# A two-block transformer on one core: the sparse attention's key split on other engines, smaller inverses, and its mask inside another product

## The chip, the cores and the metric

The kernel runs on one core of a Trainium2 chip. The metric is the device time of one execution in microseconds (us). Five engines work at the same time, each through its own list of instructions in order: TensorE (PE; its weight loads are shown as PEld), VectorE (DVE), ScalarE (ACT), GpSimd (POOL) and SyncE (SP), which here only issues DMAs. They wait for one another through semaphores.

## What is computed

Two transformer blocks on 1024 tokens of width 1024 in float32. The first has a short convolution, a retention layer and an MLP. The second has two attentions side by side, whose outputs are gated, merged and followed by another MLP. The change lies wholly in the first of the two, the sparse one; the dense one (`mla_attention`) shares its loop.

```python
def one_block(bi):                      # 128 queries, 8 heads of 64; keys and values shared by the heads
    dots = einsum('bqhd,bsd->bqhs', iqb, ikf) * IDX_DIM ** -0.5
    score = where(causal, einsum('bqh,bqhs->bqs', iwb, relu(dots)), -inf)
    _, sel = top_k(score, 256)
    k_sel, v_sel = take_rows(k, sel), take_rows(v, sel)
    bias = rel_table[rel_bucket(posq[:, :, None] - take_rows(positions, sel))]
    logits = einsum('bqhd,bqkd->bqhk', qb, k_sel) * A_HEAD_DIM ** -0.5 + swapaxes(bias, 2, 3)
    logits = where(valid[:, :, None, :], logits, NEG_INF)
    p = softmax(logits, axis=-1)
    return einsum('bqhk,bqkd->bqhd', p, v_sel)
```

The kernel does not gather: it takes the product of the queries with all keys, adds -1e30 where a key was not selected, and goes on as in a dense attention.

## The kernel before

**The loop.** Both attentions run as one loop over 128 tiles, n = 0 to 127 (`ATT`). Tiles 0 to 63 are the dense attention: for each of four pairs of heads (a round of 16 tiles), the eight query blocks b of 128 queries, two heads each. Tiles 64 to 127 are the sparse one: for each query block b, eight tiles of 16 queries by 8 heads (128 rows); a tile is 128b + 16(r + 1) keys wide, r = 0 to 7. Tile n = 64 + 8b is the first of block b.

**One tile**, by engine, each engine in its own order:
- TensorE at step n: `logits(n + 1)` into two PSUM banks (after exp n - 1 has freed them and, for the sparse ones, after the comparisons of n + 1 are there), at odd n `attend_pair((n - 3) // 2)`, then `probs_t(n)`, the transposition of the probabilities (after exp n).
- VectorE: at n >= 64 `steps_of(n + 1)`, four comparisons of the positions (`STEP`, line 2425) from which TensorE makes the relative bias; at odd n `sums_inverted` (line 2397), the inverses of two tiles' row sums; the row maximum of tile n (`NMX`, line 2464); every fourth n `attended_scaled`, which scales the finished outputs (`YB` line 2406, `YA` line 2416).
- ScalarE: exp of tile n with its row sums (line 1765), the copy of the transposed probabilities of n - 1 (line 1746), every fourth n the copy `RBS` of the spread inverses (line 1753).

**Sparse logits** (lines 1297 to 1305). The float32 product is made of float32r parts. `QS` holds for each of 64 query tiles the high parts in rows 0 to 63 and the low parts in rows 64 to 127. `KHH` holds the high parts of the keys twice, `KLO` the low parts twice. Each chunk of up to 512 keys takes three products: QS with KHH, QS with KLO, and the selection `SELB` with the mask `MB` (both bfloat16), which brings the -1e30 of a query to its 8 heads. Then follow 12 products for the bias, of 32 columns of weights each.

**Setting up the sparse part.** At its step n = 52 (`KEYS_AT`) VectorE waits until 48 tiles have logits (the keys' tiles lie where heads 0 to 5 were), copies `AKB` into both halves of KHH (lines 2450, 2451), subtracts for both halves of KLO (line 2454), and makes the comparisons of tile 64. GpSimd moves the queries into QS: after the logits of tile 47 three quarters of them (`s_aq`; two subtractions, line 849, and two copies, line 853), after those of tile 63 the rest (`s_aq2`). TensorE's `logits(64)` waits for the keys (`s_kparts`) and for `s_aq`. GpSimd has nothing else to do in the loop.

**Inverses.** `sums_inverted` writes each of two row-sum columns 64 times side by side, a 128x128 tile `RINV`, and TensorE transposes that (line 862, `RINV`) at the end of `attend_pair`, so that the inverses stand along the columns, those of the first tile in PSUM rows 0 to 63, those of the second in 64 to 127.

## Time and profile before

| | |
|---|---|
| three runs | 2951.71, 2955.83, 2956.42 us (median 2955.83) |
| the profiled execution | 2956.02 us, of which span of the trace 2954.2 us |
| PE busy | 2833.2 us, 96% of the span |
| DVE busy | 1550.5 us, 52% |
| POOL busy | 1011.7 us, 34% |
| ACT busy | 721.1 us, 24% |
| dense attention, tiles 0 to 63 | 1648 to about 1821 us |
| sparse attention, tiles 64 to 127 | about 1821 to 2030 us |

The span in 40 slices of 73.9 us; each digit is the busy share of a slice in tenths, PEclk the granted TensorE clock in tenths:

```profile
PE   7999999999999999999999996999899999999997
DVE  4853234643333324657999457996454333333337
ACT  5001124432011113453211663443111100011101
PEclk9999999999999999999999997999999999999998
```

How to read it: the attention loop lies in slices 23 to 28 (counted from 1). Elsewhere VectorE is idle for more than half of the time; here it is as busy as TensorE, and the one slice with a lower clock and a less busy TensorE in the middle of the program (the 25th, 1773 to 1846 us) belongs to it.

### The profile page before, as it was taken

Reading aid. Unit: us, or ns where it says so; the run is one execution under the profiler, and the core shown is the slowest. Engines: PE = TensorE matmul, PEld = TensorE weight load, DVE = VectorE, ACT = ScalarE, POOL = GpSimd, SP = SyncE. Lnnn points to the kernel's source line nnn. Section 1 sums busy time; section 2 is a strip of 40 time slices with the busy share of each in tenths; the row PEclk is TensorE's granted clock in tenths of the full one; section 3 lists DMA queues with packets and bytes.
Section 4 is the critical chain, followed back from the end, with each engine's and each line's share of the span. In section 5 each row is a group of like instructions: output and inputs, shape, how many; then the busy total and the mean of one; then the engine's idle time right before and its main releaser. Section 6 shows DMA issues by size and latency. Waiting matters only on the chain.

```text
span 2954.2 us, 35848 instructions
## 1 busy us (share of the span) xinstructions
PE 2833.2 (96%) x14659; PEld 2262.4 (77%) x14676; DVE 1550.5 (52%) x1841; ACT 721.1 (24%) x1055; POOL 1011.7 (34%) x441
## 2 busy tenths in 40 slices
PE   7999999999999999999999996999899999999997
PEld 4888888778888887776886564566787888888886
DVE  4853234643333324657999457996454333333337
ACT  5001124432011113453211663443111100011101
POOL 1533224454444444441222113001344444444441
PEclk9999999999999999999999997999999999999998
DMA  8531113322111122352232000003311111111111
GB/s 302 190 103 38 41 43 130 91 87 85 50 50 43 49 77 87 93 161 57 61 100 79 15 1 1 2 2 108 135 43 50 43 50 50 50 48 44 50 50 64
DMA packets 253975, 208.64 MB, mean 71 GB/s; under 512 B 23051, under 2 KB 238618, under 8 KB 253466
## 3 DMA queue, kind: packets, MB, share of 16 engines
q1 hardware_dynamic: 250826, 198.50, 21.8%
q10 hardware_dynamic: 3024, 8.39, 0.7%
q8 instruction: 89, 1.46, 0.2%
q14 instruction: 36, 0.29, 0.0%
HBM read 184.84 MB, written 20.97 MB: 70 GB/s over the span
## 4 chain that ended last, share of the span: by engine, by line
PE 78%; DVE 16%; ACT 2%; issue 2%; DMA 0%; POOL 0%; SPq 0%; ACTq 0%; DVEq 0%; POOLq 0%
PE PS L1128 18%; PE PS L1138 17%; PE PS L878 13%; PE PS L1074 10%; DVE MB L2320 6%; PE PS L1090 5%; PE PS L1363 3%; PE PS L862 3%; PE PS L1281 2%; PE PS L1332 2%; DVE STEP L2425 1%; PE PS L1305 1%; PE PS L1192 1%; DVE NMX L2464 1%; PE PS L1297 0%
## 5 line engine op out<-in xcount | busy, mean ns | idle before, releaser
L754 POOL TENSOR_TENSOR WHI<-RAW,ZERO 128x1024 fp32r<-128x1024 f32 x144 | 277.1, 1924 | 1189.0 <-PE PS L1138 292.2
L767 POOL TENSOR_TENSOR WLO<-RAW,WHI 128x1024 fp32r<-128x1024 f32 x112 | 269.8, 2409 | 478.6 <-ACT WHI L1486 478.6
L756 POOL TENSOR_TENSOR WLO<-RAW,WHI 128x1024 fp32r<-128x1024 f32 x144 | 397.0, 2757 | 11.3
L878 PE MATMUL PS<-H,WHI 128*128 128x512 f32 x864 | 271.4, 395 | 10.0 <-DVE L L1820 7.9
L878 PE MATMUL PS<-L,WHI 128*128 128x512 f32 x864 | 268.3, 392 | 0.0
L878 PE MATMUL PS<-H,WLO 128*128 128x512 f32 x864 | 267.8, 391 | 0.0
L1600 ACT ACTIVATE RL<-PS 128x1024 f32<-128x1024 f32 x48 | 49.3, 1027 | 870.9 <-PE PS L1128 870.9
L2231 DVE TENSOR_TENSOR FT<-RL 128x1024 f32<-128x1024 f32 x48 | 92.8, 1934 | 316.3 <-ACT RL L1600 316.3
L1486 ACT ACTIVATE WHI<-RAW 128x1024 fp32r<-128x1024 f32 x112 | 118.7, 1060 | 468.3 <-PE PS L1074 198.2
L1074 PE MATMUL PS<-H,WHI 128*128 128x512 f32 x512 | 202.8, 396 | 2.5 <-POOL WLO L767 1.9
L1074 PE MATMUL PS<-H,WLO 128*128 128x512 f32 x512 | 200.3, 391 | 0.0
L1074 PE MATMUL PS<-L,WHI 128*128 128x512 f32 x512 | 200.1, 391 | 0.0
L878 PEld LDWEIGHTS PS<-H,WHI 128*128 128x128 f32 x864 | 161.7, 190 | 46.1 <-issue 10.7
L878 PEld LDWEIGHTS PS<-L,WHI 128*128 128x128 f32 x864 | 163.3, 189 | 34.9
L878 PEld LDWEIGHTS PS<-H,WLO 128*128 128x128 f32 x864 | 163.3, 189 | 34.6
L2320 DVE TENSOR_SCALAR_CACHE_REDUCE MB<-SCO,CAND 128x384 bf16<-128x384 f32 (+2 forms) x198 | 174.3, 943 | 1.2
L2244 DVE TENSOR_TENSOR F2SUM<-F2SUM,PS 128x2048 f32<-128x2048 f32 x28 | 64.1, 2288 | 186.4 <-PE PS L1138 186.4
L1128 PE MATMUL PS<-A2H,WHI 128*128 128x512 f32 x512 | 157.8, 389 | 1.4 <-issue 1.4
L1138 PE MATMUL PS<-F2H,WHI 128*128 128x512 f32 x512 | 157.7, 389 | 1.3 <-ACT RS L1786 1.3
L1128 PE MATMUL PS<-A2L,WHI 128*128 128x512 f32 x512 | 157.7, 389 | 0.0
L1138 PE MATMUL PS<-F2H,WLO 128*128 128x512 f32 x512 | 157.6, 389 | 0.0
L1138 PE MATMUL PS<-F2L,WHI 128*128 128x512 f32 x512 | 157.6, 389 | 0.0
(352 smaller groups left out, 5488.6 us busy)
## 6 DMA issues: line engine op xcount, KB each, us to landing
RAW<-w_fc SPq DMA_DIRECT2D x96, 512.0 KB, 3.9
RAW<-w_ff SPq DMA_DIRECT2D x64, 512.0 KB, 3.8
RAW<-w_in SPq DMA_DIRECT2D x62, 512.0 KB, 4.2
ADA<-w_ada SPq DMA_DIRECT2D x32, 512.0 KB, 5.4
RAW<-w_out SPq DMA_DIRECT2D x24, 512.0 KB, 4.0
ADA_FIRST<-w_ada SPq DMA_DIRECT2D x16, 512.0 KB, 9.4
X<-x_scratch SPq DMA_DIRECT2D x2, 4096.0 KB, 12.7
GB<-gate_scratch SPq DMA_DIRECT2D x8, 1024.0 KB, 5.3
```

The costliest lines, as they stand in the source:

```text
L754: nc.gpsimd.tensor_add(WHI[j][:, 0:n], RAW[j][:, 0:n], ZERO[:, 0:1].to_broadcast([P, n])).then_inc(s_whi, 1)
L756: nc.gpsimd.tensor_sub(WLO[j][:, 0:n], RAW[j][:, 0:n], WHI[j][:, 0:n].bitcast(F32)).then_inc(s_w, 1)
L767: nc.gpsimd.tensor_sub(WLO[w % 2][:, :], RAW[w % 2][:, :], WHI[w % 2][:, :].bitcast(F32)).then_inc(s_w, 1)
L862: return nc.tensor.transpose(dst, src, ident[0:n, 0:n])
L878: last = mm(bank(b + t), wt[:, k, :], a[:, k * S + t * HALF:k * S + (t + 1) * HALF], start=(k == 0 and n == 0), stop=(k == KC - 1 and n == 2))
L1074: last = mm(bank(w_bank(w)), wt[:, k, :], half(a, k, e), start=(k == 0 and n == 0), stop=(k == KC - 1 and n == 2))
L1090: last = mm(bank(w_bank(w) + c), wt[:, k, c * P:(c + 1) * P], half(a, k, e), start=(k == 0 and n == 0), stop=(k == 3 and n == 2))
L1128: last = mm(bank(b + t), wt[:, k, :], a[:, k * S + t * HALF:k * S + (t + 1) * HALF], start=(k == 0 and n == 0), stop=(k == KC - 1 and n == 2))
L1138: last = mm(bank(b + 2 * c + t), wt[:, k, c * P:(c + 1) * P], a[:, k * S + t * HALF:k * S + (t + 1) * HALF], start=(k == 0 and n == 0), st ...
L1486: A(WHI[w % 2][:, :], RAW[w % 2][:, :], ACT.Copy).then_inc(s_whi, 1)
L2231: V.tensor_tensor(FT[:, :], RL[i % 2][:, :], RL[i % 2][:, :], ALU.mult).then_inc(s_h32, 1)
L2320: V.tensor_scalar(mask(b), scores(b), CAND[:, b - 2:b - 1].bitcast(F32), 0.0, op, ALU.add, accum_out=REACH[:, b - 2:b - 1]).then_inc(s_dve, 1)
```

## The change

It has three parts, all in the attention loop.
1. The split of the keys goes to ScalarE, which makes both copies of the high parts before its exp of tile 52 (new semaphore `s_khh`), and to GpSimd, which makes both subtractions after the logits of tile 47 and ahead of its own move of the queries. VectorE keeps the comparisons of tile 64 at that step.
2. `sums_inverted` writes two columns of an 8-column `RINV`. TensorE spreads them with two real products, each with a column repeated 64 times as weights and the identity as the moving side, in place of one transposition.
3. For query blocks 2 to 7 the product of QS with KLO and that of SELB with MB become one: `QSEL` (the high queries of the block in rows 0 to 63, the selection in rows 64 to 127) with `KMASK` (the low keys in rows 0 to 63, 64 rows of the mask in rows 64 to 127). The product of low queries with low keys is left out for these blocks. ScalarE fills them: at steps 67 to 70 the low keys of four KMASK tiles and the selections of two QSEL tiles (8 copies), and at steps 72 + 8(b - 2) and the two after it the queries and the two mask halves of block b.

```diff
-        RINV = [region(f"RINV{j}", K0 + 12800 + 128 * j, 128) for j in range(4)]
+        RINV = region("RINV", Y0 + 7616, 8)
...
+        QSEL = [region(f"QSEL{j}", L0 + 6144 + 1024 * j, S, F32R) for j in range(2)]
+        KMASK = [region(f"KMASK{j}", K0 + 1024 * j, S, F32R) for j in range(4)]
...
-        PAIRS, PAIR_GROUPS = 64, 32
+        PAIRS, PAIR_GROUPS, KEYS_AT, QK_SETUP = 64, 32, 52, 8
...
+                        if tiles == 48:
+                            pool.wait_ge(s_khh, 2)
+                            for e in range(2):
+                                nc.gpsimd.tensor_sub(KLO[64 * e:64 * e + 64, :], AKB[0:64, :], KHH[0:64, :].bitcast(F32)
+                                                     ).then_inc(s_kparts, 1)
...
-                        pe.wait_ge(s_kparts, 4)
+                        pe.wait_ge(s_khh, 2)
+                        pe.wait_ge(s_kparts, 2)
                         pe.wait_ge(s_aq, 4)
                     if n == 112:
                         pe.wait_ge(s_aq2, 4)
-                    at = slice(i * P, (i + 1) * P)
+                    if b >= 2 and i % NB == 0:
+                        pe.wait_ge(s_qk2, QK_SETUP + 3 * (b - 1))
+                    at, own = slice(i * P, (i + 1) * P), slice((i % NB) * P, (i % NB + 1) * P)
                     for c in range(0, w, HALF):
                         cw = min(HALF, w - c)
                         mm(dst[:, c:c + cw], QS[:, at], KHH[:, c:c + cw], start=True, stop=False)
-                        mm(dst[:, c:c + cw], QS[:, at], KLO[:, c:c + cw], start=False, stop=False)
-                        mm(dst[:, c:c + cw], SELB[:, (i % NB) * P:(i % NB + 1) * P],
-                           MB[:, MASK_AT[b] + c:MASK_AT[b] + c + cw], start=False, stop=False)
+                        if b < 2:
+                            mm(dst[:, c:c + cw], QS[:, at], KLO[:, c:c + cw], start=False, stop=False)
+                            mm(dst[:, c:c + cw], SELB[:, own],
+                               MB[:, MASK_AT[b] + c:MASK_AT[b] + c + cw], start=False, stop=False)
+                        else:
+                            mm(dst[:, c:c + cw], QSEL[b % 2][:, own],
+                               KMASK[2 * (b % 2) + i % NB // 4][:, c:c + cw], start=False, stop=False)
...
-                transpose(out[:, (2 + p % 2) * P:(3 + p % 2) * P], RINV[p % 4][:, :]).then_inc(s_pv, 1)
+                for e in range(2):
+                    n = 2 * p + e
+                    last = mm(out[64 * e:64 * e + 64, (2 + p % 2) * P:(3 + p % 2) * P],
+                              RINV[:, n % 8:n % 8 + 1].to_broadcast([P, 64]), ident, start=True, stop=True)
+                last.then_inc(s_pv, 1)
...
+            def low_keys_copied(j):
+                A(KMASK[j][0:64, :], KLO[0:64, :].bitcast(F32), ACT.Copy).then_inc(s_qk2, 1)
+            def selection_copied(j, e):
+                A(QSEL[j][64:P, HALF * e:HALF * (e + 1)], SELB[64:P, HALF:S], ACT.Copy).then_inc(s_qk2, 1)
+            def queries_copied(b):
+                A(QSEL[b % 2][0:64, :], QS[0:64, b * S:(b + 1) * S].bitcast(F32), ACT.Copy).then_inc(s_qk2, 1)
+            def mask_copied(b, e):
+                w = P * (b + 1)
+                A(KMASK[2 * (b % 2) + e][64:P, 0:w], MB[64 * e:64 * e + 64, MASK_AT[b]:MASK_AT[b] + w], ACT.Copy
+                  ).then_inc(s_qk2, 1)
             for n in range(128 + 3):
+                if n == 67:
+                    act.wait_ge(s_lg, 64)
+                    act.wait_ge(s_pv, PAIRS // 2)
+                    act.wait_ge(s_kparts, 2)
+                if 67 <= n < 71:
+                    low_keys_copied(n - 67)
+                    selection_copied((n - 67) // 2, (n - 67) % 2)
+                b, step = (n - 64) // NB + 1, (n - 64) % NB
+                if 72 <= n < 120 and step < 3:
+                    if step == 0:
+                        act.wait_ge(s_lg, 64 + NB * (b - 1))
+                        if b == 6:
+                            act.wait_ge(s_aq2, 4)
+                        queries_copied(b)
+                    else:
+                        mask_copied(b, step - 1)
+                if n == KEYS_AT:
+                    act.wait_ge(s_lg, 48)
+                    for e in range(2):
+                        A(KHH[64 * e:64 * e + 64, :], AKB[0:64, :], ACT.Copy).then_inc(s_khh, 1)
...
-                V.reciprocal(RINV[p % 4][:, :].rearrange("p (e n) -> p e n", e=2),
-                             RSUM[:, at].rearrange("p (e o) -> p e o", o=1).broadcast_to([P, 2, 64])).then_inc(s_ri, 1)
+                V.reciprocal(RINV[:, at], RSUM[:, at]).then_inc(s_ri, 1)
...
-                    V.tensor_copy(KHH[0:64, :], AKB[0:64, :]).then_inc(s_kparts, 1)
-                    V.tensor_copy(KHH[64:P, :], AKB[0:64, :]).then_inc(s_kparts, 1)
-                    dve.wait_ge(s_kparts, 2)
-                    for e in range(2):
-                        V.tensor_sub(KLO[64 * e:64 * e + 64, :], AKB[0:64, :], KHH[0:64, :].bitcast(F32)).then_inc(s_kparts, 1)
                     steps_of(64)
```

## Rows read from the trace of the kernel before

**Rows 1.** Stretches: us, busy PE, PEld, DVE, ACT, POOL; clock; DMA share, GB/s.

```profile
1700.00:1750.00 50.00, 48.45 (x378) 33.08 (x377) 27.74 (x38) 30.70 (x69) 0.00 (x0) 1.00 0.01 1
...
1856.20:1897.40 41.20, 35.92 (x398) 21.33 (x398) 40.57 (x105) 18.24 (x52) 0.00 (x0) 1.00 0.01 2
1897.40:1951.00 53.60, 52.54 (x711) 37.67 (x721) 52.98 (x104) 25.06 (x52) 0.00 (x0) 1.00 0.01 2
1951.00:2020.50 69.50, 69.50 (x836) 46.51 (x840) 64.81 (x102) 32.22 (x52) 0.00 (x0) 1.00 0.01 2
```

**Rows 2.** The chain that ended last, by line: 1856-1876, then 1951-2020 us.

```profile
by line: DVE STEP L2425 48.6%; DVE RINV L2397 22.4%; DVE NMX L2464 13.3%; issue 10.2%; DVE YA L2416 7.9%; DVEq L2463 0.2%
...
by line: PE PS L1305 29.0%; PE PS L862 23.1%; PE PS L1332 19.5%; PE PS L1297 12.2%; PE PS L1298 9.6%; PE PS L1299 6.9%
```

**Rows 3.** Timeline of VectorE around the key split: start, us, instructions.

```profile
1772.22 4.07 DVE L2450 CAST KHH<-AKB 64x1024 fp32r<-64x1024 f32 x1
1782.04 7.46 DVE L2454 TENSOR_TENSOR KLO<-AKB,KHH 64x1024 fp32r<-64x1024 f32 x2
```

**Rows 4.** Chain in order of time, one shape in three dense rounds.

```profile
1702.59 1.08 PE PS L1281 x4
...
1740.52 1.08 PE PS L1281 x4
...
1798.58 1.08 PE PS L1281 x4
```

**Rows 5.** Stretches for TensorE alone: us, busy, count, granted clock, DMA.

```profile
1790.00:1795.00 5.00, 3.24 (x12) 0.50 0.00 0
1840.00:1845.00 5.00, 4.89 (x42) 0.50 0.01 3
1850.00:1855.00 5.00, 4.07 (x53) 1.00 0.00 0
```

**Rows 6.** Timeline of GpSimd, and of TensorE at the first sparse tile.

```profile
1762.29 13.46 POOL L849 TENSOR_TENSOR QS<-AQP,AQH 64x3072 fp32r<-64x3072 f32 x2 [72.89 <-PE PS L1284]
1775.82 11.35 POOL L853 TENSOR_TENSOR QS<-AQH,ZERO 64x3072 fp32r<-64x3072 f32 x2
...
1820.83 0.26 PE L1297 MATMUL PS<-KHH,QS 128*128 128x16 f32 x1
```

**Rows 7.** ScalarE groups: busy, mean ns, idle before (second: 1897-2020 us only).

```profile
L1773 ACT ACTIVATE H<-YA 128x1024 fp32r<-128x1024 f32 x4 | 3.9, 1044 | 1.3 <-DVE YA L2416 1.3
...
L1765 ACT ACTIVATE PB<-PS,NMX 128x512 f32<-128x512 f32 (+31 forms) x32 | 28.6, 895 | 64.5 <-DVE NMX L2464 64.5
```

**Rows 8.** VectorE: a reciprocal, the work behind it, and a four-column group.

```profile
1936.47 0.96 DVE L2397 RECIPROCAL RINV<-RSUM 128x128 f32<-128x128 f32 x1
1937.33 0.87 DVE L2464 TENSOR_REDUCE NMX<-PS 128x1 f32<-128x736 f32 x1
...
L2025 DVE RECIPROCAL RS<-SS 128x4 f32<-128x4 f32 x8 | 1.4, 175 | 15.0 <-ACT SS L1493 15.0
```

**Rows 9.** Chain pieces of TensorE, and the group of a spread.

```profile
2002.04 1.02 PE PS L862 x8
...
2005.66 1.90 PE PS L1332 x32
2007.55 1.13 PE PS L862 x9
...
L892 PE MATMUL PS<-IDN,RS 128*128 128x128 f32 x80 | 11.6, 306 | 0.6 <-DVE RS L1815 0.6
```

**Rows 10.** Chain pieces of one tile's mask products, block 6.

```profile
1977.08 0.23 PE PS L1299
...
1977.61 0.15 PE PS L1299
```

**Rows 11.** VectorE's comparisons during GpSimd's last move of queries, and after it.

```profile
1828.41 4.50 DVE L2425 TENSOR_SCALAR STEP<-POSB,THR 128x48 bf16<-128x48 f32 x4
...
1835.35 0.73 DVE L2425 TENSOR_SCALAR STEP<-POSB,THR 128x64 bf16<-128x64 f32 x4
```

More of the change, by code:

```diff
@@ L384, in build @@
         s_rbc = sem("probability_sum_inverse_spread")
-        s_aqh, s_kparts = sem("query_high_parts"), sem("shared_keys_split")
+        s_aqh, s_khh, s_kparts = sem("query_high_parts"), sem("shared_keys_high_part"), sem("shared_keys_low_part")
         s_aq2 = sem("last_queries_moved")
         s_c4, s_aq, s_tpd = sem("tables_in"), sem("queries_moved"), sem("tables_ready")
+        s_qk2 = sem("queries_and_mask_copied")
         s_tab, s_tp = sem("bias_table_in"), sem("bias_steps_product")
@@ L2426, in steps_of @@
                                     None, ALU.is_le).then_inc(s_step, 1)
-            TABLES_AT, KEYS_AT = 14, 52
+            TABLES_AT = 14
             for n in range(128):
```

## The prediction, made before the changed kernel was run

> **What bounds the kernel now.** I read the page first: TensorE is busy nearly everywhere, and the one stretch where VectorE is as busy lies in the attention loop, so I asked for busy times by stretch there, then for the chain by line, and last for the timelines around the key split. In the dense part TensorE is busy 48.45 of 50 us and VectorE 27.74 [rows 1]: TensorE bounds it. In query blocks 2 and 3 VectorE is busy 40.57 of 41.2 us [rows 1] and the chain consists of VectorE's lines alone, 22.4% of it the inverses [rows 2]. In blocks 4 and 5 both engines are full: 52.54 and 52.98 of 53.6 us. In blocks 6 and 7 TensorE is busy all of the time and the chain is wholly its own [rows 1, 2]; VectorE, at 64.81 of 69.5, is close behind. So there VectorE's saving is worth something only as far as TensorE's goes.
>
> **Part 1, the key split.** VectorE begins it at 1772.2 and is through at 1789.5 [rows 3]; meanwhile no tile gets a row maximum. What this costs in all, the restart included, is seen where one shape of TensorE's work returns each round: 1702.6 to 1740.5 is 37.9 us, 1740.5 to 1798.6 is 58.1 [rows 4]. The difference is 20.1 us, and it holds the slow restart (granted clock 0.50, its 1.2 GHz level, after 17 us without work) [rows 5]. All of it goes: **-20.1**.
> What comes in its place:
> - ScalarE makes two copies of 1024 columns before exp 52, at 1.04 us each by its copy from SBUF [rows 7], 2.1 us. Behind them in its queue stand exp 52 and the copy of the transposed probabilities 51, for which TensorE waits. Exp 52 would wait some 0.5 us anyway for the comparisons and the maximum ahead of it: **+1.6**. Range 0.5 to 2.1.
> - GpSimd can start only when the copies are there, at 1772.2 + 0.5 + 2.1 = 1774.8 instead of 1762.3 [rows 6]. Its two subtractions are taken from its own of the same kind: 13.46 us for 2 x 3072 columns is 2.2 us for 1024, so 4.5. The move of the queries follows, 13.46 + 11.35 = 24.8 [rows 6]. End: 1774.8 + 29.3 = 1804.1. TensorE came to the first sparse tile at 1820.8 [rows 6]; now that is 1820.8 - 20.1 + 1.6, and 0.8 for the inverses of six pairs (part 2), 1803.1. It waits about a microsecond and a semaphore: **+1.5**. Behind that wait in TensorE's queue stand the attended pair 30 and the last dense transposition. Range 0 to 6.
> Net of part 1: -17.0.
>
> **Part 2, the inverses.** On VectorE the 128-column reciprocal occupies 0.86 us, from its start to that of the next instruction [rows 8]. For two columns the nearest row is the group of four columns, 0.175 us [rows 8]; less the same overlap of 0.1 us it occupies under 0.1. So 0.77 us is saved for each pair of tiles. On TensorE a transposition goes and two real products come, each in two passes. The transposition costs 1.13 - 1.02 = 0.11 us (nine against eight in the chain) [rows 9]. For the new ones there are two bounds. The attended products have the same form (64 columns of weights, 128 moving, halves of the output in turn), 1.90 us for 32 instructions [rows 9], 0.06 each, 0.24 for four: +0.13 a pair. The spread of a reciprocal root has the same operands but the full width, 11.6 us for 80 instructions [rows 9], 0.145 each, 0.58 for four: +0.47. I take +0.13, since the halves of the output are what makes instructions run beside each other in the attended row, and keep 0.47 for the range.
>
> **Part 3, the mask.** Each chunk of blocks 2 to 7 loses a bfloat16 product. Its share in the chain is 0.23 us for 512 keys and 0.15 for a rest of some 300 [rows 10], about what its columns take; a rest of 70 or 200 keys gets 0.1, 0.12 by estimate from these. The product that stays has the same size and type as the one with KLO. ScalarE gets the copies: 4 x (1.04 + 0.5) us at tiles 67 to 70, and for each block 1.04 and two of 0.4 to 1.0 at three tiles. In blocks 4 to 7 it sits idle 64.5 us in front of 32 exps, 2.0 each [rows 7], and a copy stands exactly there, before an exp that waits for its maximum. The longest is 1.04, and even with 0.4 us less idle time per tile it is covered: taken at nothing for blocks 2 to 7. Were the cover gone, it would be 6 x 1.04 + 9 = 15 us in all.
>
> **The stretches of the sparse part.**
> - Blocks 0 and 1. GpSimd's second move of queries stays as it is and holds VectorE's comparisons as before (four in 4.50 us against 0.73) [rows 11]. After it the clock is at 0.50 with TensorE busy 4.89 of 5 us, and back at 1.00 by 1850 [rows 5]. Until then TensorE bounds, VectorE's saving is worth nothing, the added products cost double, and ScalarE's 1.5 us per tile at 67 to 70 lies on a loop with little room: +1.0. The three pairs behind gain 2, of which I take 1.5. Together **-0.5**, range +3 to -4 (if the clock doesn't fall).
> - Blocks 2 and 3, bound by VectorE: 8 pairs x 0.77 = 6.2, of which other waits may take some: **-5.5**.
> - Blocks 4 and 5: VectorE would come to 52.98 - 6.2 = 46.8, TensorE to 52.54 - 16 x 0.33 + 8 x 0.13 = 48.3 [rows 1]. The larger sets the end: 53.6 - 48.3, **-5.3**. Range -3 to -6.
> - Blocks 6 and 7, TensorE: 8 x 0.38 + 8 x 0.45 = 6.6 less 8 x 0.13, **-5.6**. VectorE at 64.81 - 6.2 = 58.6 stays below 69.5 - 5.6 = 63.9.
> - Dense part: 32 x 0.13 = 4.2 on TensorE; a little falls into its waits: **+3.0**.
>
> Behind the loop nothing is touched. **Sum**: -17.0 + 3.0 - 0.5 - 5.5 - 5.3 - 5.6 = -30.9. The profiled execution took 2956.0 us, 0.2 above the median of the runs, so 2925.1; I say **2925**.
>
> **The rivals.**
> A. *GpSimd becomes what the sparse part waits for.* If its subtractions run like VectorE's did (7.46 for two) [rows 3] the move ends 3 us later, and the comparisons of tile 65, which VectorE wants just then, are held as in rows 11, 2 us more. Against it: its own subtraction is measured at 2.2. Time: 2925 + 5 = 2930. Chance 0.12. The Trainium skill (SBUF — State Buffer, Who interferes with whom) says that VectorE's copies and tensor-scalar forms with both ports and GpSimd's instructions lock each other out for a whole instruction. The trace agrees: a copy of 64x1024 took 4.07 us beside GpSimd [rows 3]. By that rule the comparisons of 65 wait for the end of GpSimd's last copy, which is this rival's second part.
> B. *The inverses' products don't overlap.* At +0.47 instead of +0.13, 0.34 more on the 32 dense pairs and the 16 of blocks 4 to 7, 16 us: 2941. For it: the row with the same operands. Against it: the row with the same shape. Chance 0.08.
> C. *The clock stays low: slower than before.* TensorE loses work and waits at the first sparse tile. If the clock falls there and stays at 0.50, TensorE's work takes twice as long. Blocks 2 and 3 hold 35.9 us of it [rows 1], less some 2.6 for the masks, plus 1.0: 34.3, doubled 68.6 against the 35.7 forecast, +33. Block 4 holds about 22 of the 48.3, by width, +21. The point is where the extra reaches 31 us, at the end of block 3; through block 4 it is 2925 + 54 = 2979. Against it: at 4.07 busy of 5 us the clock came back to 1.00 [rows 5], and stayed there through blocks 2 and 3 at 35.92 of 41.2 [rows 1]. Chance 0.03. The Trainium skill (TensorE: Matmul & The Clock Gate, Part 4: PE-mode transpose) holds that transpositions don't count as work for the clock as products do. The change removes products and leaves the transpositions, which speaks for this rival; in exchange 64 transpositions become products. No row here tells the two kinds apart.
> D. *ScalarE's copies aren't hidden.* With VectorE faster, exp is reached sooner and the loop from maximum to exp to transposition to logits closes without slack; then half of the 15 + 6 us shows: 2935. Chance 0.10.
> E. *The change doesn't do what it says*: the inverses weren't what bounds blocks 2 to 5, because TensorE's chain of logits, exp and transposition is as long. Then of 10.8 us half comes: 2930. Chance 0.07.
>
> **How the numbers follow.** Forecast 0.60, A 0.12, B 0.08, C 0.03, D 0.10, E 0.07. The forecast's own range, from the spreads above (-4 to +6 around 2925), is 2918 to 2933. The range of 8 in 10 takes in A, D and E and most of B: **2914 to 2940**; its low end is the clock that doesn't fall after the second move and the smaller ends of the added waits together. What a measurement of this kernel can tell from no change is about 0.2%, 6 us. Everything but C is faster by more than that; of C half ends within it or is a gain: faster 0.96, same 0.01, slower 0.03.
>
> **What would show it.** Right: no idle of TensorE around tile 52; ScalarE's copies there of 1.04 us each, GpSimd's subtractions of 2.2; a wait of TensorE at the first sparse tile of 1 to 2 us; VectorE's reciprocal under 0.2 us; blocks 2 and 3 in some 36 us, 4 and 5 in 48, 6 and 7 in 64; a low clock after GpSimd's second move. Wrong: a dense round of more than 39 us (B), exps that start right behind a copy of ScalarE (D), blocks 2 to 5 with VectorE idle (E), or a clock of 0.50 in them (C). The prediction fails most easily where the two engines are equally full, since there each small wait on one shows on the other.

## The result

The changed kernel takes 2922.77 us (median of four runs, 2922.09 to 2922.97) against 2953.77 for the kernel before in the same comparison (four runs, 2951.69 to 2956.42). The ratio is 0.9893 with a 95% interval of 0.9877 to 0.9909: 31.0 us less, between 26.9 and 36.3 by the interval. The prediction was 2925 with 2914 to 2940 around it.

To see where it went, the loop is cut at the starts of row maxima, which both kernels have. These are the first maxima of blocks 0, 2, 4 and 6 and the last of all in the changed kernel's timeline of VectorE (start, us, line, form):

```profile
1804.23 0.16 DVE L2512 TENSOR_REDUCE NMX<-PS 128x1 f32<-128x16 f32 x1
...
1840.26 0.44 DVE L2512 TENSOR_REDUCE NMX<-PS 128x1 f32<-128x272 f32 x1
...
1877.51 0.71 DVE L2512 TENSOR_REDUCE NMX<-PS 128x1 f32<-128x528 f32 x1
...
1929.08 0.97 DVE L2512 TENSOR_REDUCE NMX<-PS 128x1 f32<-128x784 f32 x1
...
1988.89 1.22 DVE L2512 TENSOR_REDUCE NMX<-PS 128x1 f32<-128x1024 f32 x1 [3.62 <-PE PS L1320]
```

The same division of every run's timeline gives the table on which the rest stands (us; "rounds" are tiles 16 to 31 and 32 to 47, "split round" tiles 48 to 63, where the keys are split; the last column ends at the maximum of tile 127):

| kernel | rounds | split round | blocks 0, 1 | blocks 2, 3 | blocks 4, 5 | blocks 6, 7 | tiles 16 to 127 |
|---|---|---|---|---|---|---|---|
| before | 38.0, 37.9 | 58.9 | 37.2 | 42.0 | 54.8 | 64.6 | 333.3 |
| changed | 38.7, 38.5 | 42.5 | 36.0 | 37.3 | 51.6 | 59.8 | 304.3 |
| e1, split only | 38.0, 37.9 | 41.8 | 37.2 | 42.0 | 54.8 | 64.6 | 316.3 |
| e2, inverses only | 38.7, 38.5 | 58.8 | 36.1 | 38.8 | 54.5 | 65.6 | 330.9 |
| e3, mask only | 38.1, 37.9 | 58.9 | 38.2 | 42.1 | 54.8 | 61.6 | 331.6 |
| e4, no block copies | 40.1, 38.5 | 42.5 | 35.5 | 37.7 | 51.6 | 59.8 | 305.7 |
| e5, copy first | 38.3, 38.5 | 42.5 | 35.1 | 37.3 | 51.6 | 59.8 | 303.0 |
| e6, late wait | 38.2, 38.5 | 42.5 | 35.0 | 37.2 | 51.6 | 59.8 | 302.7 |
| e7, maximum between | 38.7, 38.5 | 42.5 | 34.9 | 40.0 | 55.1 | 64.9 | 314.5 |
| e8, setup moved | 38.7, 38.5 | 40.7 | 36.3 | 37.3 | 51.6 | 59.8 | 302.9 |
| e9, spread | 38.3, 38.5 | 40.8 | 31.6 | 37.6 | 50.4 | 59.7 | 296.8 |
| e10, two bias parts | 38.7, 38.5 | 42.5 | 36.0 | 37.3 | 49.4 | 56.7 | 298.9 |
| e11, narrow comparison | 38.2, 38.5 | 42.5 | 35.0 | 37.5 | 50.1 | 59.4 | 301.3 |
| e12, combined | 37.9, 37.9 | 40.6 | 33.5 | 37.6 | 50.4 | 59.7 | 297.6 |

Stretches without an edit repeat within 0.1 us at most places. The first round and blocks 0 and 1 do not, and the granted clock of stretches of 1 us shows why: at these two places TensorE's clock is low for a time that differs from run to run. About the start of the first round it was low for 3 us in the changed kernel, e2, e7, e8 and e10 (38.7 us each), for 7 us in e4 (40.1) and not at all in e5, e6, e9 and e11 (38.2 or 38.3). In blocks 0 and 1, behind GpSimd's second move, it was low for 17 us in the kernel before and e1 (37.2 both), for 14 in the changed kernel, e2 and e10 (36.0 and 36.1), and for 10 in e5, e6, e7 and e11 (34.9 to 35.1). From its first maximum to its last the loop is 28.2 us shorter (372.4 before, 344.2 now). The other 5 us by which the two profiled spans differ (2954.2 and 2921.0) lie outside it, in instructions that the change does not touch: over all the runs the loop's first maximum starts anywhere between 1642.9 us (e10) and 1650.9 us (e1), and what follows the last maximum takes 932 to 934.

**After, by stretch** (blocks 2 and 3, 4 and 5, 6 and 7; columns as in rows 1). VectorE is no longer full in blocks 2 and 3 (35.82 of 37.2), in 4 and 5 neither is full, and in 6 and 7 TensorE nearly is:

```profile
1840.30:1877.50 37.20, 34.43 (x430) 21.79 (x430) 35.82 (x104) 23.45 (x58) 0.00 (x0) 1.00 0.01 2
1877.50:1929.10 51.60, 49.91 (x735) 38.35 (x735) 48.68 (x105) 31.22 (x58) 0.00 (x0) 1.00 0.01 2
1929.10:1988.90 59.80, 59.11 (x758) 41.70 (x757) 53.58 (x92) 32.54 (x51) 0.00 (x0) 1.00 0.01 2
```

**The prices of parts 2 and 3**, as the group of VectorE's reciprocals and pieces of TensorE's chain in block 7 (start, us, what). The reciprocal is down from 0.96 us to 0.156 [rows 8]. The two real products with `RINV` (L1353) take 0.22 us, and a chunk has two products of 0.23 where it had three [rows 10]. VectorE's busy time falls by less than the reciprocals' own times say, since they overlap their neighbours: from 41.3 to 35.9 us in blocks 2 and 3 with part 2 alone (e2), 0.7 us a pair.

```profile
L2451 DVE RECIPROCAL RINV<-RSUM 128x2 f32<-128x2 f32 x64 | 10.0, 156 | 1.6 <-ACT PB L1819 1.5
...
1974.68 1.90 PE PS L1347 x32
1976.58 0.22 PE PS L1353 x4
1976.80 1.03 PE PS L870 x8
1977.83 0.24 PE PS L1308
1978.06 0.23 PE PS L1314
```

**The split round.** The timeline at tile 52 (what the instruction waited for in brackets), and TensorE by stretch (columns as in rows 5):

```profile
1770.96 2.13 ACT L1809 ACTIVATE KHH<-AKB 64x1024 fp32r<-64x1024 f32 x2
...
1773.11 0.58 ACT L1819 ACTIVATE PB<-PS,NMX 128x384 f32<-128x384 f32 x1
1773.25 4.76 POOL L852 TENSOR_TENSOR KLO<-AKB,KHH 64x1024 fp32r<-64x1024 f32 x2 [86.95 <-ACT KHH L1809]
...
1774.20 0.87 PE L870 MATMUL PS<-IDN,PB 128*128 128x128 f32 x3 [1.72 <-ACT RAW L1765]
```

```profile
1770.00:1775.00 5.00, 3.28 (x22) 0.91 0.00 0
1775.00:1780.00 5.00, 5.00 (x27) 0.74 0.00 0
1780.00:1785.00 5.00, 5.00 (x37) 1.00 0.01 3
```

The exp of tile 52 stands behind the two copies, TensorE waits 1.72 us, and its clock falls again, though for a short time: its mean is 0.91 and then 0.74, some 3 us at 0.50, against 20 us in the kernel before. It fell there in all eight kernels with both copies in one place, and in none of the three that set them apart (e8, e9, e12). And here is GpSimd's chain, with TensorE's first sparse product:

```profile
1777.98 13.49 POOL L857 TENSOR_TENSOR QS<-AQP,AQH 64x3072 fp32r<-64x3072 f32 x2
1791.54 10.68 POOL L861 TENSOR_TENSOR QS<-AQH,ZERO 64x3072 fp32r<-64x3072 f32 x2
...
1802.56 0.26 PE L1308 MATMUL PS<-KHH,QS 128*128 128x16 f32 x1
```

It ends at 1802.2, and TensorE, whose first sparse tile starts at 1802.56 right behind its transpositions, does not wait at all. The margin is 0.3 us.

### The profile page after: what moved, and what is told of

It reads as the page before. It is cut to its first block, busy times and chain, and to the rows that moved or that the text cites. A ratio compares the mean times of both kernels' runs of the same rounds, so it can differ in the third digit from the quotient of the medians.

```text
span 2921.0 us, 36119 instructions
## 1 busy us (share of the span) xinstructions
PE 2813.7 (96%) x14788; PEld 2256.0 (77%) x14788; DVE 1483.3 (51%) x1837; ACT 745.3 (26%) x1083; POOL 1014.9 (35%) x443
## 4 chain that ended last, share of the span: by engine, by line
PE 79%; DVE 15%; ACT 3%; issue 2%; DMA 0%; POOL 0%; SPq 0%; ACTq 0%; DVEq 0%; POOLq 0%
PE PS L1136 18%; PE PS L1146 17%; PE PS L886 14%; PE PS L1082 10%; DVE MB L2374 6%; PE PS L1098 5%; PE PS L1382 3%; PE PS L870 3%; PE PS L1289 2%; PE PS L1347 2%; PE PS L1320 1%; DVE STEP L2478 1%; DVE NMX L2512 1%; PE PS L1200 1%; PE PS L1261 1%
## 5 line engine op out<-in xcount | busy, mean ns | idle before, releaser
L2285 DVE TENSOR_TENSOR FT<-RL 128x1024 f32<-128x1024 f32 x48 | 92.8, 1934 | 316.3 <-ACT RL L1619 316.3
L2512 DVE TENSOR_REDUCE NMX<-PS 128x1 f32<-128x128 f32 (+26 forms) x128 | 92.8, 725 | 128.4 <-PE PS L1292 113.4
L1136 PE MATMUL PS<-A2H,WLO 128*128 128x512 f32 x512 | 157.6, 389 | 0.0
## 6 DMA issues: line engine op xcount, KB each, us to landing
X<-x_scratch SPq DMA_DIRECT2D x2, 4096.0 KB, 12.7
```

Of the source, the lines that this page charges most:

```text
L1136: last = mm(bank(b + t), wt[:, k, :], a[:, k * S + t * HALF:k * S + (t + 1) * HALF], start=(k == 0 and n == 0), stop=(k == KC - 1 and n == 2))
L2285: V.tensor_tensor(FT[:, :], RL[i % 2][:, :], RL[i % 2][:, :], ALU.mult).then_inc(s_h32, 1)
L2512: V.reduce_max(NMX[:, n % 2:n % 2 + 1], bank(2 * (n % 2), 2)[:, 0:w], AX, negate=True).then_inc(s_nm, 1)
```

## The experiments

**Each part alone** (three kernels, each the kernel before with the edits of one part of the diff).

e1, the split only:

> The kernel before with part 1 alone: keys' split on ScalarE and GpSimd, inverses and mask as before. Theory (the stall of the split was worth 20.1 us, and what comes in its place is ScalarE's two copies and a slow restart): the round of dense tiles that holds the split falls from 58.1 to about 41.2 us, every other stretch stays within 0.5 us, total 16 to 17 us below before, 2937. Rival (part of the gain of that round comes from the smaller inverses, since they leave VectorE free at the restart): 12 to 14 us, 2941.

2938.04 us, ratio 0.9944 (0.9927 to 0.9960), 16.5 us below the kernel before. In the table the split round falls by 17.0 us, and no other stretch moves by more than 0.1. Against the changed kernel's 42.5 the round is even 0.7 shorter, since the dense tiles have no added products. The theory holds and its rival falls.

e2, the inverses only:

> The kernel before with part 2 alone: two-column inverses. Theory (VectorE and TensorE bound by turns, so parts 2 and 3 are worth more together than apart): dense part +2.2 us (0.56 a round), blocks 2 and 3 -4.5, blocks 4 and 5 -1.5, blocks 6 and 7 +0.8; in all 2 to 4 us faster, 2951. Rival (the parts add up: each stretch's gain is the sum of its parts'): blocks 4 to 7 gain at least 1.5 us in all from this part, and with the next run's they come to the 8.0 of the whole change.

2951.35 us, 0.9990 (0.9980 to 1.0001). Rounds +0.7 and +0.5, the split round 0, blocks 2 and 3 -3.2, 4 and 5 -0.3, 6 and 7 +1.0. The theory has the signs right, but expected 4.5 in blocks 2 and 3 and 1.5 in 4 and 5; its rival, that the parts add up, falls. e3, the mask only:

> The kernel before with part 3 alone: the mask inside the low keys' product. Theory: nothing in blocks 2 and 3, where VectorE bounds (0 to -0.5), -1.5 in blocks 4 and 5, -4.5 in blocks 6 and 7 (down to VectorE's busy time), and up to +1 in blocks 0 and 1 for ScalarE's setup copies; in all 5 to 6 us faster, 2948. Rival (parts add up): blocks 4 to 7 gain 6.5 or more.

2953.60 us, 0.9993 (0.9984 to 1.0003). Blocks 2 to 5 don't move (42.1, 54.8), 6 and 7 fall by 3.0, and blocks 0 and 1 grow by 1.0, where ScalarE makes its setup copies. Expected were 1.5 in blocks 4 and 5, 4.5 in 6 and 7 and 5 to 6 us in all, so here too either part alone was worth less than thought. Neither part alone is clear of no change. Against these two the whole change gives:

| | blocks 2, 3 | blocks 4, 5 | blocks 6, 7 |
|---|---|---|---|
| inverses alone | -3.2 | -0.3 | +1.0 |
| mask alone | +0.1 | 0.0 | -3.0 |
| their sum | -3.1 | -0.3 | -2.0 |
| together (changed kernel) | -4.7 | -3.2 | -4.8 |

That is 7.3 us of the 12.7 that appear only when both are there. The parts do not add up: one takes time from VectorE, the other from TensorE, and in blocks 4 and 5, where both are full before [rows 1], either alone is worth nothing.

**Why blocks 4 and 5 gave 3.2 us and not the 5.3 forecast.** In the changed kernel neither engine is full there (TensorE 49.91, VectorE 48.68 of 51.6 us). First ScalarE's copies, rival D of the prediction:

> The changed kernel without ScalarE's copies of queries and mask for blocks 4 to 7, whose products then read the tiles of blocks 2 and 3 (those blocks' mask copies are made 1024 columns wide so that all columns are filled); the logits of blocks 4 to 7 are therefore not the real ones. Theory (ScalarE's copies are covered; the loop from maximum to exp to copy to transposition limits blocks 4 to 7 without them too): blocks 4 to 7 stay within 1 us of the changed kernel's 51.6 and 59.8 us, total 2922 to 2923. Rival D (the copies delay exps): blocks 4 and 5 fall by 1.5 to 2 us, 6 and 7 by about 1, total 2920.

```diff
...
-                w = P * (b + 1)
+                w = S
...
-                if 72 <= n < 120 and step < 3:
+                if 72 <= n < 88 and step < 3:
```

Blocks 4 to 7 take 51.6 and 59.8 us, as with the copies; total 2922.54, ratio 0.9892 (0.9875 to 0.9908). The block copies cost nothing there. (Blocks 2 and 3, whose mask copies are made wider in this run, take 37.7 us instead of 37.3.) Next the loop that the changed kernel's timeline in block 5 suggests:

```profile
1911.53 1.24 DVE L2469 TENSOR_TENSOR YA<-PS,RBS 64x128 f32<-64x128 f32 x4
...
1915.01 0.87 DVE L2512 TENSOR_REDUCE NMX<-PS 128x1 f32<-128x688 f32 x1
...
1915.91 0.83 ACT L1819 ACTIVATE PB<-PS,NMX 128x688 f32<-128x688 f32 x1 [2.60 <-DVE NMX L2512]
...
1916.74 0.80 ACT L1765 ACTIVATE RAW<-PS 128x768 f32<-128x768 f32 x1
...
1917.68 0.85 PE L870 MATMUL PS<-IDN,PB 128*128 128x128 f32 x6 [0.37 <-ACT RAW L1765]
```

ScalarE waits 2.60 us for a maximum, then makes exp and the copy of the tile before, and only then TensorE transposes. Two theories: the copy in that place (L1), or VectorE's order, where the maximum stands behind the comparisons (L2).

> The changed kernel with one order turned on ScalarE in the sparse part: at odd tiles n the copy of the transposed probabilities of n - 1 stands before exp n instead of behind it, in the time in which ScalarE waits for the maximum of n. Theory L1 (in blocks 4 to 7 the loop maximum, exp, copy, transposition, logits is what limits, with the copy's 0.8 us in it): these blocks fall from 51.6 and 59.8 us by 1.5 us each, total 2920. Theory L2 (VectorE's own order limits, where the maximum of n stands behind the four comparisons of n + 1): no change, within 0.5 us in each; total 2922 to 2923.

```diff
+                if n > 64 and n < 128 and n % 2:
+                    probs_copied(n - 1)
                 if n < 128:
                     act.wait_ge(s_nm, n + 1)
...
-                if 0 <= n - 1 < 128:
+                if 0 <= n - 1 < 128 and not (n > 64 and n < 128 and n % 2):
                     probs_copied(n - 1)
```

2922.57 us, 0.9886 (0.9861 to 0.9910); blocks 4 to 7 unchanged to 0.01 us. L1 falls: the 0.37 us that the bracket shows is no price.

> The changed kernel with TensorE's wait for the comparisons moved behind the products of the logits, before the bias products, which alone read them. Theory L2 (VectorE's order limits: TensorE stands waiting for comparisons at the start of the logits): blocks 2 and 3 fall by 2 us from 37.3, 4 and 5 by 1.5, 6 and 7 by 0.5; total 2918 to 2919. Theory L1 (exp and copy limit): blocks 2 and 3 by 1 at most, blocks 4 to 7 unchanged; total 2922.

```diff
-                    pe.wait_ge(s_step, NSTEP * (n - 63))
...
+                    pe.wait_ge(s_step, NSTEP * (n - 63))
                     for c in range(0, w, HALF):
                         cw = min(HALF, w - c)
                         for part in range(3):
```

2923.91 us, 0.9893 (0.9870 to 0.9915); again nothing moves from block 2 on. TensorE does not lose time by waiting early for the comparisons, and L2, which expected a gain, misses.

> As the late wait for the comparisons, and on VectorE the maximum of tile n stands between the first two and the last two comparisons of n + 1 instead of behind all four, so that exp n starts about 1.1 us earlier in block 5. Theory L2: blocks 4 and 5 fall by 3 us from 51.6, 6 and 7 by 2 to 3 from 59.8, total 2915. Theory L1 gives part of it too, since exp starts earlier, but less than the run with the copy first plus 1. Rival (TensorE is full in blocks 6 and 7): 6 and 7 unchanged within 0.5, total 2920.

```diff
                 if n >= 64 and n + 1 < 128:
-                    steps_of(n + 1)
+                    steps_of(n + 1, 0 if split else None)
...
                 V.reduce_max(NMX[:, n % 2:n % 2 + 1], bank(2 * (n % 2), 2)[:, 0:w], AX, negate=True).then_inc(s_nm, 1)
+                if split:
+                    steps_of(n + 1, 1)
```

2933.52 us, 0.9927 (0.9903 to 0.9952): slower by 2.7, 3.5 and 5.1 us in the three pairs of blocks. Both theories foresaw a gain, so both miss. The waits between 1886 and 1996 us of this run, in blocks 4 to 7 (who waited for whom, us in total, times, longest), show why: the comparisons stand behind a maximum that waits for TensorE, and TensorE's bias products then wait for them.

```profile
PEld PS L1320 <- DVE STEP L2478: 14.6, 24, 1.1
DVE NMX L2513 <- PE PS L1320: 10.5, 17, 1.5
PE PS L1320 <- DVE STEP L2478: 8.7, 16, 0.7
```

Each engine waits for the other within one tile; in the changed kernel the same view has no wait of TensorE for `STEP`. So of the two orders the one before is the better: four comparisons ahead of the maximum keep VectorE busy while TensorE works.

Then theory S, that both engines are nearly full and lose to unevenness. Two runs take work from one engine at a time.

> The changed kernel with two of the three bias parts in blocks 4 to 7 (the middle part of the bias is left out), which takes 0.24, 0.30, 0.35 and 0.40 us of each tile from TensorE and nothing from VectorE. Theory S (both nearly full): blocks 4 and 5 fall by 1 to 2 of the 4.3 us taken out, 6 and 7 by 3 to 5 of 6.0. Rival V (VectorE alone limits blocks 4 and 5): 0 there. Rival T (TensorE alone): 4.3.

```diff
-                        for part in range(3):
+                        for part in range(3) if n < 96 else (0, 2):
```

> The changed kernel with the fourth of VectorE's comparisons 16 columns wide from tile 98 on (the bias of a quarter of the queries in blocks 4 to 7 is therefore made from old comparisons), which takes 0.29, 0.36, 0.42 and 0.49 us of each tile from VectorE and nothing from TensorE. Theory S: blocks 4 and 5 fall by 2 to 3 of the 5.2 us taken out, 6 and 7 by 0.5 to 1.5 of 7. Rival V: 5.2 in blocks 4 and 5. Rival T: nothing in any.

```diff
+                    if n >= 96 and g == 3:
+                        w = S if n < 98 else 16
```

TensorE's busy time fell by 3.8 us in blocks 4 and 5 and 5.9 in 6 and 7 with the first edit (estimated were 4.3 and 6.0), VectorE's by 5.0 and 6.1 with the second (5.2 and 7; at tiles 96 and 97 that edit makes the comparison wider). With less on TensorE, blocks 4 and 5 fall by 2.2 of the 3.8 us, 6 and 7 by 3.2 of 5.9. With less on VectorE, 4 and 5 fall by 1.5 of 5.0, 6 and 7 by 0.4 of 6.1. There is one run of each (2917.02 and 2921.77 us); the stretches carry the verdict. Neither V nor T holds: in blocks 4 and 5 somewhat over half of TensorE's saving and less than a third of VectorE's is realised, so both set the pace. S has the kind right and the sizes only roughly: it expected 1 to 2 us and 2 to 3 there. The third run takes no work away and only spreads a bunch.

> The changed kernel with (a) the moves of the last such run, but the eight setup copies one to a tile (tiles 67 to 71 and 75 to 77), and (b) VectorE's four output products of a group of four sparse tiles (1.24 us in one piece every fourth tile) spread over four tiles, one each. Theory S (in blocks 4 to 7 both engines are nearly full and lose to unevenness, the bunch of products being one): blocks 4 and 5 fall from 51.6 by 1 to 2 us, block 6 a little, blocks 2 and 3 by 0.5; blocks 0 and 1 from 36.0 to about 34; total 2918. Rival (the sums per tile decide, not their order): blocks 2 to 7 unchanged within 0.3.

```diff
-                if n >= 7 and n % 4 == 3:
+                if n >= 7 and n % 4 == 3 and n < 71:
                     attended_scaled((n - 7) // 4)
+                if n >= 71:
+                    attended_scaled((n - 7) // 4, (n - 7) % 4)
...
```

2914.66 us, ratio 0.9869 (0.9852 to 0.9886). Blocks 4 and 5 fall from 51.6 to 50.4 with the same work in another order, and there TensorE is full (columns as in rows 1):

```profile
1871.42:1921.82 50.40, 50.26 (x738) 38.39 (x736) 49.39 (x106) 31.06 (x59) 0.00 (x0) 1.00 0.01 2
```

S holds there; 6 and 7 together stay (59.7), being TensorE's, and blocks 2 and 3 do not gain but lose 0.4, which S had not foreseen. The larger gain of this run is ahead of block 2, with e8:

> The changed kernel with three moves ahead of block 2: ScalarE's two copies of the keys' high parts stand two tiles apart (before exps 50 and 52); the copies of the last quarter of the queries' high parts go from GpSimd to ScalarE (before exp 66); the eight setup copies stand at tiles 75 to 78 instead of 67 to 70. Theory: the clock fell at tile 52 because ScalarE held exp 52 for 2.1 us, so the round of the split comes from 42.5 to 40.5 us or less; blocks 0 and 1 fall by 2 to 4 us from 36.0, because GpSimd's lock on VectorE's comparisons ends 3.9 us sooner; total 2917 to 2919. Rival: the clock falls again at both places for the wait that is left, and under 2 us is gained in all, 2921.

```diff
-                if n == KEYS_AT:
+                if n in (KEYS_AT - 2, KEYS_AT):
...
+                if n == 66:
...
+                        A(to[0:64, :, e, :], piece(AQH, e).bitcast(F32), ACT.Copy).then_inc(s_aq2, 1)
...
-                if 67 <= n < 71:
+                if 75 <= n < 79:
```

2924.19 us, 0.9896 (0.9873 to 0.9918). The split round falls from 42.5 to 40.7 us, and TensorE by stretch shows the clock at 1.00 where it was 0.74; at the second place, behind GpSimd's second move, it falls as before:

```profile
1775.00:1780.00 5.00, 4.21 (x29) 1.00 0.00 0
1815.00:1820.00 5.00, 5.00 (x64) 0.50 0.01 3
```

Both the theory (2917 to 2919 us in all) and its rival (the clock falls at both places) are half right: the first place gained 1.8 us, blocks 0 and 1 together nothing. Moving the copies of the last queries shortens block 0 from 20.6 to 18.1 us (four comparisons beside GpSimd take 2.85 us there instead of 4.50), but block 1 grows from 15.4 to 18.3. The timeline names the cause: two setup copies stand before one exp, and TensorE, by then at full clock, waits for what comes behind it:

```profile
1833.98 1.05 ACT L1775 ACTIVATE KMASK<-KLO 64x1024 fp32r<-64x1024 f32 x1
...
1834.24 0.41 PE L870 MATMUL PS<-IDN,PB 128*128 128x128 f32 x2 [1.04 <-ACT RAW L1765]
...
1835.06 0.63 ACT L1778 ACTIVATE QSEL<-SELB 64x512 fp32r<-64x512 bf16 x1
```

So rival D was real, but in blocks 0 and 1, where two copies are 1.7 us a tile. In e9, with the same moves, one copy a tile and VectorE's products spread from tile 71 on, blocks 0 and 1 take 31.6 us instead of 36.3; how much of it each of the two edits gives was not tried. Last, what the dense part pays:

> The run e9_spread with two more edits: the dense tiles keep the inverses of the kernel before (128-column reciprocals, one transposition), the sparse tiles the two-column ones; and the output products are spread only up to tile 122, so that block 7 has them in one piece again. Theory (in the dense part TensorE bounds and pays the added products): each dense round falls from 38.5 to 37.9 us, 2.2 us in all; block 7 from 29.7 to 29.0; total about 2912. Rival (the rest of the program's clock decides more than this): the total stays at 2914 to 2915, while the stretches fall.

```diff
+                if p < 32:
+                    transpose(out[:, (2 + p % 2) * P:(3 + p % 2) * P], RINVW[p % 4][:, :]).then_inc(s_pv, 1)
+                    return
...
```

2918.14 us, beside 2957.17 for the kernel before in that comparison; ratio 0.9864 (0.9847 to 0.9880), by the ratios 1.5 us better than e9 and within its interval. The dense rounds are back at 37.9 as foreseen. Block 7 stays at 29.7 where 29.0 were expected, so its 0.7 us in e9 (block 6 gained as much) did not come from the spread products. Blocks 0 and 1 took 33.5 with the same edits as in e9's 31.6, and the timeline shows a difference right at their start: TensorE waits at the first sparse tile for GpSimd's copies, which end at 1799.8.

```profile
1789.15 10.68 POOL L862 TENSOR_TENSOR QS<-AQH,ZERO 64x3072 fp32r<-64x3072 f32 x2
1799.98 0.25 PE L1309 MATMUL PS<-KHH,QS 128*128 128x16 f32 x1 [1.53 <-DVE STEP L2494]
```

The bracket names the comparisons, but those of tile 64 had long been made; the wait ends 0.15 us behind GpSimd. After it the clock was at 0.50 for 3 us. In e8 and e9 the wait at this place is 1.1 us, and the clock stays at 1.00. So the wait that the prediction feared for the changed kernel came as soon as the split round was 2 us shorter. e9 and e12 are the fastest of the set by their ratios, 0.24% and 0.29% below the changed kernel; the intervals overlap, which is why the stretches, not the totals, are the evidence.

## Why the prediction came out

In the total it was 2 us off; the gain forecast was 30.9 us, the medians differ by 31.0 and the loop alone by 28.2. Term by term (between the maxima of the table above, so that blocks 6 and 7 hold 15 of their 16 tiles):

| step of the prediction | forecast | measured |
|---|---|---|
| the stall goes, and ScalarE's copies come | -20.1 + 1.6 = -18.5 | -17.0 (e1: the split round 58.9 to 41.8) |
| wait for GpSimd at the first sparse tile | +1.5 | 0 |
| dense inverses, four rounds | +3.0 | +2.4 (0.6 a round, from two rounds of e2) |
| blocks 0 and 1 | -0.5 | -1.1 |
| blocks 2 and 3 | -5.5 | -4.7 |
| blocks 4 and 5 | -5.3 | -3.2 |
| blocks 6 and 7 | -5.6 | -4.8 |

- *The stall.* It went as a whole; of the net, 1.5 us are missing. If the 20.1 read from three rounds [rows 4] is right, the replacement costs 3.1 us and not 1.6: the step counted ScalarE's 2.1 us less what exp 52 waits anyway, but not that the clock falls once more after so short a gap. e8, which sets the two copies two tiles apart, gets 1.8 us of it back and keeps the clock at 1.00. It makes the wait shorter too (0.79 us instead of 1.72), so how much of the 1.8 is the clock's is not shown. Of the signs named, "no idle of TensorE around tile 52" did not come.
- *GpSimd.* From the first subtraction to the end of the move it took 29.0 us, 29.3 were forecast (subtractions 2.34 each instead of 2.2, copies 10.68 instead of the 11.35 of [rows 6]). TensorE came to the first sparse tile 29.3 us after GpSimd's start where 28.3 were reckoned, its clock having been low for 3 us on the way, and the microsecond by which GpSimd would have been late was gone. So this term came out at nothing by 0.3 us, through the very delay that the step before had missed: that is luck. Where the clock didn't fall (e8, e9, e12), TensorE waited 1.1 to 1.5 us there, as forecast. Rival A fell in the changed kernel. Its second half, the lock, is real: in those three runs the comparisons of tile 65 stood beside GpSimd's last copy and took 1.6 to 2.0 us instead of 0.88, and with GpSimd's later copies moved away (e8) four comparisons took 2.85 us instead of 4.50. The Trainium skill (SBUF — State Buffer, Who interferes with whom) has such instructions of VectorE and GpSimd exclude each other for a whole instruction; the trace agrees (four comparisons in 4.50 us beside GpSimd, against 0.73 without it [rows 11]).
- *The inverses.* Of the two bounds, the attended row was the right one (0.24 forecast, 0.22 measured [rows 9]), the spread's 0.58 was not, and rival B fell. The reciprocal is 0.8 us shorter, but VectorE's busy time fell by only 0.7 us a pair (e2), 5.5 us in blocks 2 and 3 where 6.2 were reckoned.
- *Blocks 0 and 1.* The low clock after GpSimd's second move came back in the same place, as said, for 14 us instead of 17. The -1.1 is about as large as that stretch's own variation: e10 and e11, whose code is the changed kernel's up to block 4, take 36.0 and 35.0, with the clock low for 14 and 10 us behind that move. Whether the change made the low stretch shorter is open.
- *Blocks 2 and 3.* VectorE-bound, as said, and 0.8 us short: VectorE is now busy 35.82 of 37.2 us and no longer alone in setting the pace.
- *Blocks 4 and 5.* This is the mis-sized term. The step took the larger of the two engines' remaining busy times as the new length. Two engines that depend on each other tile by tile do not reach it by themselves. Between the maxima of the table TensorE was busy 54.3 of 54.8 us before and is busy 49.9 of 51.6 now. The work taken off it is about the 4.2 forecast, but it stands idle for 1.7 us where the step had none. e9 recovers 1.2 of them by evening out VectorE's work and ends with TensorE full (50.26 of 50.40), and e10 and e11 show that in the changed kernel both engines still count. Another 0.6 us was never there: the prediction read its stretch from 1897.4 to 1951, where TensorE was idle for 1.1 us, and between the blocks' maxima it was idle for 0.5.
- *Blocks 6 and 7.* 0.41 us a tile in block 7 (31.9 to 29.0 over seven tiles), about the mask's price, but only 0.24 in block 6. That the same unevenness acts there is likely, since block 6 falls from 30.8 to 30.0 in e9 with TensorE full; but block 7 grows by 0.7 in that run, and why is open.
- *The sum* of these misses is small because they have both signs: 1.5 us too hopeful in the split and 3.7 from block 2 on, 2.7 too cautious in the wait for GpSimd, the dense inverses and blocks 0 and 1. The further 3 us by which the medians gained more than the loop are as much as unchanged code varies, so the closeness of the total is partly luck. Two of the prediction's own figures do not fit each other: spreads of -4 to +6 around 2925 are 2921 to 2931 and not 2918 to 2933, and with all but C faster the chance of faster is 0.97 at least, not 0.96. Rival C did not occur: in blocks 2 to 7 the clock is 1.00. In e3 it fell for 3 us in block 2, and the stretch, bound by VectorE, did not grow (42.1). That transpositions count less for the clock, which the Trainium skill holds (TensorE: Matmul & The Clock Gate, Part 4: PE-mode transpose), is shown by no run here, in either direction. Of rival E there is a trace: in e2, with the wide inverses gone from VectorE, blocks 2 and 3 gave 3.2 us of 5.5, and 4.7 with part 3 beside it.

## What to carry to other kernels

Where two engines are both full, price an edit of either alone at nothing and of both together at less than the larger of the remaining busy times says, until the work of each is spread evenly over the tiles (e9). Try such edits as a pair, since each alone looks like no change (0.999 here, against 0.989 for all three parts). When a burst of work moves to an idle engine, look at what is queued behind it there and put it in pieces of one per turn of the loop: the same copies made TensorE wait up to a microsecond a tile in pairs (e8), and with one to a tile (and the products spread) blocks 0 and 1 were the shortest of all runs (e9, e12). When one wait is removed, look for the next one within a microsecond of it: GpSimd, 0.3 us ahead in the changed kernel, was late by 1.1 to 1.5 in e8, e9 and e12. And before blaming a wait in a bracket, take it away: two orders that the timeline suggested were worth 0.0 us.

## What was not expected of the hardware

- TensorE's clock fell from its 2.4 GHz to its 1.2 GHz level after a wait of 1.72 us at tile 52 (it was busy 4.08 us of the 5 from 1765 to 1770 us, and 3.28 of the next 5), and not in e8, where it was busy 3.57, 5.00 and 4.21 in the three stretches from 1765 us. A wait of 1.53 us at the first sparse tile came before a fall (e12), waits of 1.1 there did not (e8, e9). In the sparse part a wait of 3.2 us and one of 1.6 (e8) both came before a fall to 0.50, which lasted from 10 us (e9) to 17 (before), by the mean clock of stretches of 1 us.
- The same instructions do not always meet the same clock: in the first round it fell in ten of the fourteen runs and not in the other four, and in e10 it fell also at 1806 us, where in the changed kernel, with the same code up to there, it did not (blocks 0 and 1 took 36.0 us in both).
- VectorE's narrow reciprocal of two columns takes 0.156 us, against 0.175 for four [rows 8], so nearly all of it is not for the columns.
- The same unchanged work ahead of the loop, some 1643 to 1651 us, ends up to 8 us apart from kernel to kernel, while blocks 4 to 7 repeat within 0.02 us in the changed kernel, e5, e6 and e8.
